# Five reorderings in a two-block model kernel: a state copy, modulation tiles, gb's halves and held loads

## The chip, the cores and the metric

The kernel runs on one core of a Trainium2 chip. The metric is the device time of one launch in microseconds (us); three runs of the kernel before gave 926.8, 927.32 and 931.11, so the median is 927.32 us.

## The reference, cut to what matters

A sequence of 256 tokens of width 1024 goes through three layers. The first is an even mixer (a gated depthwise convolution of 31 taps, layer-normed, beside a gated linear recurrence, LRU, in both directions), the second an odd mixer (pooling over windows of 2, 4, 8 and 16 in rows of 64, grouped matmuls, a gate). The third is a block with its own inputs: chunked HGRN2 attention in both directions, a gated MLP over positions (SGU), then a SwiGLU. All is fp32.

```
for l in range(DEPTH):
    shift, scale, gate = split(silu(c) @ mod_w[l] + mod_b[l], 3)
    hx = modulate(rmsnorm(x, norm_g[l]), shift, scale)
    ...                                  # even_mixer or odd_mixer
    x = x + gate * out_x
# second block
p = h @ w_in                             # f_f, f_b, i, q, og, u, v, ga, gb
o_f, s_f = hgrn2_chunked(qh, k_f, logf_f, vh, s0_f)      # s0: the context's final state
o_b, s_b = hgrn2_chunked(flip(...), s0_b)
o_b_mlp = chunk_sgu(gelu(u), gelu(v), ln_v_g, ln_v_b, w_s, b_s)   # uses layernorm(v)
merged = sigmoid(ga) * (o_a @ w_pa) + sigmoid(gb) * (o_b_mlp @ w_pb)
x = x + mod[2] * (merged @ w_o)
x = x + mod[5] * ((silu(a) * b) @ w_down)                # a, b = split(h2 @ w_up)
out = rmsnorm(x, g_final)
```

The state is carried from chunk to chunk as S = diag(decay) S + d, four chunks of 64 tokens in each direction, and starts from the state that the context leaves.

## The kernel before, in words

Features lie on the partitions, the 256 tokens along the free axis. All weights are one stream of 252 tiles of 128 rows by 1024 columns (512 KB), in the order of `ORDER` (line 72). A tile is named after its product: `xb`, `va`, `vg`, `gate`, `cv`, `ga`, `gb`, `ya`, `yb` in the first layer, `ou`, `og`, `grp`, `oa`, `ob` in the second, `f`, `i`, `q`, `u`, `v`, `o`, `ga2`, `gb2`, `pa`, `pb`, `wo`, `ua`, `ub`, `d0` to `d2` in the third. A tile of most names passes through four engines:

- SyncE loads it into `raw`, a ring of six (line 413), once TensorE has finished the tile six places earlier.
- ScalarE rounds it to `w_hi` (`highs`, line 956), VectorE takes the remainder as `w_lo` (`lows`, line 1370). Both are called by name and index at fixed places of each engine's program and work off all tiles up to the one named.
- TensorE does three matmuls of 256 columns for each of the eight k-tiles (`three`, lines 573 to 575), 24 to a tile, and moves on. `tile_done` counts the tiles.

Each engine's program is written out by hand and runs strictly in order, so a VectorE instruction that waits holds up all that stand behind it, the next `w_lo` too. There is no scheduler; the semaphores alone tie the engines.

The modulation vectors of the later layers (`mod`) are made on VectorE: GpSimd loads 80 tiles `modw` of 512 KB in groups of four (line 452), each slot again when `modw_used` tells that VectorE is done with it; `mod_tiles(g, row, first, n)` (line 1399) multiplies tiles of group g with a row and sums (line 1404).

The places of the change:

- First layer, ga: `lru_root(3, ...)` and `lru_scan(3)` are the recurrence of the last pair of heads, with `lows` for the tiles ga 4 to ga 7 inside.
- First layer, gb: VectorE normalises the convolution (`normalised`), multiplies it with ga (`ya_product`, line 1647) and splits it (`ya_low`, line 1651), beside ScalarE's `conv_silu` and `ya_high`.
- Second layer, ou: TensorE computes ou 0 to 3 side by side, so that these four are finished within a short time and four loads go out together. ScalarE copies each product to `opad` (line 1201), VectorE pools four of them at a time (`pooled`), and multiplies modulation tiles twice (`second_pair`).
- Third layer, the second direction (d = 1): TensorE makes the context's state in `px[0]` (`context_state`, line 802); VectorE copies it to `St` (line 1957). Only then may TensorE write the transposed keys into `px[0]` (`keys(1, 0)`, line 794), which ScalarE copies out (line 1271). Chunk states follow (line 814), then `scores` (line 824). `normalise_v` (from line 1998) is the layer norm of v for the SGU and stands between `decays(1)` and `states(1)`.
- Third layer, up: `mod_tiles(18, 0)` stands ahead of the loop over the 22 pairs ua, ub.

Of the kernel before, what the change touches and what calls it, by code (L numbers as in the profile page):

```python
# [72 lines left out]
TILE = {key: n for n, key in enumerate(ORDER)}  # L73
# [78 lines left out]
def build(nc, ins, out):  # L152
    with ExitStack() as ctx:
# [14 lines left out]
        gb2 = at("gb2", 68, [KT, T])  # L168
# [107 lines left out]
        ga2 = at("ga2", W, [KT, T])  # L276
# [167 lines left out]
        def _(pool):  # L444
# [34 lines left out]

            copies_after = {3: (0,), 5: (1,), 7: (2, 3), 11: (4, 5), 15: (6,), 17: (7,)}  # L480
            for g in range(MOD_TILES // MOD_SLOTS):
                if g == 17:
                    pool.wait_ge(sg_act, 1)
                    add_up([(vn[:, 0, :], v2), (vsq[:, 0, :], vsq)], sg_act, 0, HEADS, 0)
                elif g == 19:
                    add_up([(sq4[:, 0, :], sq4)], sq_ready, 4 * KT, KT - 1)
                for n in range(g * MOD_SLOTS, (g + 1) * MOD_SLOTS):
                    loads(n)
                    for t in copies_after.get(n, ()):
                        shifted_copies(t)  # L490
                if g == 7:
                    add_up([(sq1[:, 0, :], sq1)], sq_ready, 0, KT - 1)
                elif g == 10:
                    add_up([(sqx[:, 0, :], sqx)], sq_ready, KT, KT - 1)
                elif g == 12:
                    add_up([(sq2[:, 0, :], sq2), (sqc[:, 0, :], sqc)], sq_ready, 2 * KT, KT - 1, 2)
# [447 lines left out]
        def _(act):  # L944
# [100 lines left out]
            def silu_out(name, t, dst):  # L1045
                done(name, t)
                act.activation(dst[:, t, :], psum_of(name, t)[:, 0:T], ACT.Silu).then_inc(free_of(name, t), 1)
# [119 lines left out]
            silu_out("gb", 0, gb)  # L1167
            conv_silu(0)
            silu_out("gb", 1, gb)
            conv_silu(1)  # L1170
            ya_high(0)
            ya_high(1)
# [187 lines left out]
        def _(v):  # L1360
# [241 lines left out]
            mod_tiles(3, 1, 2, 2)  # L1602
            lru_scan(2)
            lows("ga", 3)
            mod_tiles(4, 1)
            lru_root(3, ("ga", 5))
            lows("ga", 7)
            mod_tiles(5, 1, 0, 2)
            lru_scan(3)
            lows("gb", 2)  # L1610
            mod_tiles(5, 1, 2, 2)
            mods_used(6)
# [54 lines left out]
            normalised(1)  # L1667
            lows("gb", 5)
            ya_product(0)
            ya_product(1)  # L1670
            v.wait_ge(lru_free, KT)
            yb_product(0, 2)
            lows("gb", 6)
            ya_low(0)
            lows("gb", 7)
            ya_low(1)
# [274 lines left out]
            def states(d):  # L1951

                g0_ = 4 + 10 * d
                order = (0, 1, 2, 3) if d == 0 else (3, 2, 1, 0)
                lows(*(("v", 1) if d == 0 else ("ga2", 5)))
                v.wait_ge(hg_pe, g0_ + 3)
                v.tensor_copy(St[:, order[0], :, :], px[0][:].rearrange("p (h e) -> p h e", h=HEADS)).then_inc(hg_dve, 1)
                for n in range(3):
                    lows(*(("v", 3) if d == 0 else ("ga2", 7)) if n == 0 else (("o", 0) if d == 0 else ("gb2", 0)))
                    v.wait_ge(hg_pe, g0_ + 6 + n)  # L1960
                    if n:
                        S.sync()
                    v.wait_ge(hg_dve, 9 * d + 5 + n)
                    for hd in range(HEADS):
                        c = hd * CHUNKS + order[n]
                        a = v.scalar_tensor_tensor(out=St[:, order[n + 1], hd, :], in0=St[:, order[n], hd, :],
                                                   scalar=dec[:, c:c + 1], in1=px[n % 2][:, hd * P:(hd + 1) * P],
                                                   op0=ALU.mult, op1=ALU.add)
                        if hd == HEADS - 1:
                            a.then_inc(hg_dve, 1)  # L1970
                        else:
                            S.do(a)
                lows(*(("o", 2) if d == 0 else ("gb2", 1)))
                v.wait_ge(hg_pe, g0_ + 9)
                v.wait_ge(in_sgu, 48)
                mask = tri[:, d:d + 1, :].to_broadcast([P, HEADS, P])
                S.do(v.copy_predicated(sc[:, 0:HEADS, :], mask, px[0][:].rearrange("p (r t) -> p r t", t=P)))
                S.sync()
                v.copy_predicated(sc[:, HEADS:, :], mask, px[1][:].rearrange("p (r t) -> p r t", t=P)) \
                 .then_inc(hg_dve, 1)  # L1980
# [12 lines left out]

            def normalise_v():

                lows("ga2", 2)
                v.wait_ge(sd_ready, 8)
                S.do(v.reciprocal(lnv[:, 1, :], lnv[:, 3, :]))
                S.sync()
# [1 line left out]
                def by_token(a):  # L2001
                    return a.rearrange("p (n t) -> p n t", n=1).to_broadcast([P, HEADS, T])

                lows("ga2", 3)
                S.do(tt_(vn[:], v2[:], by_token(lnv[:, 0, :]), ALU.subtract))
                S.sync()
                S.do(tt_(vn[:], vn[:], by_token(lnv[:, 1, :]), ALU.mult))
# [13 lines left out]
            mod_tiles(16, 0)  # L2021
            lows("o", 2)
            decays(1)
            normalise_v()
            states(1)
            mod_tiles(17, 0)

# [74 lines left out]
            rstd(10, v4[:, 0, :], v4[:, 1, :])  # L2102
            modulate(3 * KT, x, v4[:, 1, :], sc3, sh3, t4, h3_hi, h3_lo)
            lows("ub", 2)
            mod_tiles(18, 0)
            for t in range(FT):
                ahead("ua", t)
                emptied(v, "ua", t)
# [4 lines left out]
                S.do(v.tensor_copy(ff_hi[:, t, :], fr))  # L2113
                S.sync()
                v.tensor_tensor(ff_lo[:, t, :], fr, ff_hi[:, t, :].bitcast(F32), ALU.subtract).then_inc(ff_ready, 1)
                if 2 <= t < 6:
                    mod_tiles(19, 0, t - 2, 1)
            mods_used(20)
            S.do(tt_(gate3, mod[:, 9 * KT:10 * KT], col("b_mod_2", 5 * KT, KT), ALU.add))
            S.sync()  # L2120
# [101 lines left out]
```

## Time and profile before

| | before |
|---|---|
| median of three runs | 927.32 us |
| the profiled execution: its own time | 927.22 us |
| its span, first to last instruction | 925.4 us |
| TensorE busy | 893.5 us, 97% of the span |
| VectorE busy | 701.2 us, 76% |
| ScalarE busy | 501.5 us, 54% |
| GpSimd busy | 143.1 us, 15% |
| HBM read | 188.60 MB, 205 GB/s over the span |
| mean granted TensorE clock | 0.993 |

The span is 1.8 us less than the time; that rest lies around it. TensorE's share is high, and matmuls are pipelined, so what counts is where it stands idle and where its clock was lowered: the few stretches of idle time, and who ended each.

### The profile page before, as it was taken

The page shows a single profiled execution, that of the slowest core. Times are in us where ns is not written, and L with a number is a line of the kernel's source. Part 1 is how long each engine was busy: PE and PEld are TensorE (multiplying, and loading weights), DVE is VectorE, ACT ScalarE, POOL GpSimd, SP SyncE. Part 2 cuts the span into 40 slices and gives each one's busy share as a digit, 9 for nine tenths or more (in the row PEclk, how much of TensorE's full clock was granted, in tenths as well). Part 3 has the DMA queues.
Part 4 walks back from the last instruction along what each step waited for, and adds up shares of the span by engine and source line. Part 5 has one row for each costly group of instructions (what it writes and reads, how often), then busy time and mean ns, then how long its engine had stood idle before and what let it go on. Part 6 is the DMA issues. An engine that isn't in the chain of part 4 may idle for free.

```text
span 925.4 us, 17444 instructions
## 1 busy us (share of the span) xinstructions
PE 893.5 (97%) x7172; PEld 838.2 (91%) x7172; DVE 701.2 (76%) x1008; ACT 501.5 (54%) x718; POOL 143.1 (15%) x254
## 2 busy tenths in 40 slices
PE   8999999999999999999999999979999999999996
PEld 7788777689999999989999999969999889999995
DVE  5687578989798999878589975776985786666453
ACT  5475888896744555335544483654544354444441
POOL 0004674710022003200311100300001000000000
PEclk9999999999999999999999999989999999999999
DMA  9934977986685878866628754625565375565661
GB/s 369 369 137 150 313 261 223 276 315 195 199 274 183 299 236 257 296 207 183 185 89 335 243 154 122 224 73 183 169 183 175 136 249 183 183 182 183 201 197 58
DMA packets 55294, 195.44 MB, mean 211 GB/s; under 512 B 7856, under 2 KB 7984, under 8 KB 53808
## 3 DMA queue, kind: packets, MB, share of 16 engines
q1 hardware_dynamic: 39600, 147.73, 49.0%
q0 software_dynamic: 15616, 46.61, 14.7%
q8 instruction: 57, 0.93, 0.4%
q14 instruction: 21, 0.17, 0.1%
HBM read 188.60 MB, written 1.05 MB: 205 GB/s over the span
## 4 chain that ended last, share of the span: by engine, by line
PE 65%; DVE 16%; DMA 6%; ACT 5%; issue 4%; POOL 2%; SPq 0%; DVEq 0%; ACTq 0%; POOLq 0%
PE ps L573 19%; PE ps L575 18%; PE ps L574 18%; DVE w_lo L1370 6%; PE ps L734 3%; DMA raw<-in_stream 2%; DMA m<-in_mod_w 2%; ACT w_hi L956 2%; DMA modw<-in_mod_w 2%; POOL shifts L461 2%; PE px L652 2%; PE ps L663 1%; DVE modw L1404 1%; DVE win L1384 1%; DVE li L1384 1%
## 5 line engine op out<-in xcount | busy, mean ns | idle before, releaser
L1370 DVE TENSOR_TENSOR w_lo<-raw,w_hi 128x1024 fp32r<-128x1024 f32 x232 | 281.0, 1228 | 113.2 <-ACT w_hi L956 112.8
L956 ACT ACTIVATE w_hi<-raw 128x1024 fp32r<-128x1024 f32 x232 | 243.1, 1055 | 114.7 <-DMA raw<-in_stream 113.7
L573 PE MATMUL ps<-h_hi,w_hi 128*128 128x256 f32 (+1 forms) x928 | 274.8, 296 | 13.8 <-DVE w_lo L1370 10.8
L574 PE MATMUL ps<-h_lo,w_hi 128*128 128x256 f32 (+1 forms) x928 | 270.1, 291 | 0.0
L575 PE MATMUL ps<-h_hi,w_lo 128*128 128x256 f32 (+1 forms) x928 | 270.1, 291 | 0.0
L573 PEld LDWEIGHTS ps<-h_hi,w_hi 128*128 128x128 f32 x928 | 178.3, 192 | 24.8 <-DVE w_lo L1370 13.7
L574 PEld LDWEIGHTS ps<-h_lo,w_hi 128*128 128x128 f32 x928 | 178.5, 192 | 3.6 <-issue 1.2
L575 PEld LDWEIGHTS ps<-h_hi,w_lo 128*128 128x128 f32 x928 | 178.4, 192 | 2.6
L573 PE MATMUL ps<-h2o_hi,w_hi 128*128 128x256 f32 x352 | 102.1, 290 | 0.0
L574 PE MATMUL ps<-h2o_lo,w_hi 128*128 128x256 f32 x352 | 100.1, 284 | 0.0
L575 PE MATMUL ps<-h2o_hi,w_lo 128*128 128x256 f32 x352 | 100.0, 284 | 0.0
L452 POOL DMA_DIRECT2D modw<-in_mod_w x80 | 42.8, 537 | 331.3 <-DVE modw L1404 187.4
L1404 DVE SCALAR_TENSOR_TENSOR modw<-modw,c_row 128x1024 f32<-128x1024 f32 x64 | 76.3, 1227 | 7.5 <-DMA modw<-in_mod_w 7.5
L461 POOL DMA_DIRECT2D shifts<-upad x128 | 62.7, 498 | 62.0 <-DVE upad L1523 56.1
L573 PEld LDWEIGHTS ps<-h2o_hi,w_hi 128*128 128x128 f32 x352 | 68.1, 193 | 0.8 <-issue 0.2
L574 PEld LDWEIGHTS ps<-h2o_lo,w_hi 128*128 128x128 f32 x352 | 68.0, 193 | 0.3 <-issue 0.2
L575 PEld LDWEIGHTS ps<-h2o_hi,w_lo 128*128 128x128 f32 x352 | 68.0, 193 | 0.0
L474 POOL TENSOR_TENSOR sq<-sq 128x256 f32<-128x256 f32 x24 | 19.4, 810 | 309.4 <-ACT sq L1185 309.4
L1185 ACT ACTIVATE sq<-x 128x256 f32<-128x256 f32 x32 | 13.4, 418 | 67.6 <-DVE x L1693 67.4
L573 PE MATMUL ps<-ff_hi,w_hi 128*128 128x256 f32 x176 | 49.8, 283 | 0.0
L574 PE MATMUL ps<-ff_lo,w_hi 128*128 128x256 f32 x176 | 49.8, 283 | 0.0
L575 PE MATMUL ps<-ff_hi,w_lo 128*128 128x256 f32 x176 | 49.8, 283 | 0.0
(336 smaller groups left out, 1761.8 us busy)
## 6 DMA issues: line engine op xcount, KB each, us to landing
raw<-in_stream SPq DMA_DIRECT2D x252, 512.0 KB, 3.8
modw<-in_mod_w POOLq DMA_DIRECT2D x80, 512.0 KB, 5.8
m<-in_mod_w SPq DMA_DIRECT2D x8, 1024.0 KB, 19.4
shifts<-upad POOLq DMA_DIRECT2D x128, 35.5 KB, 3.9
c_row<-in_c_rows SPq DMA_DIRECT2D x3, 512.0 KB, 6.6
ctxT<-in_ctxT SPq DMA_DIRECT2D x1, 1024.0 KB, 4.9
x<-in_xT SPq DMA_DIRECT2D x1, 1024.0 KB, 6.9
ctx2T<-in_ctx2T SPq DMA_DIRECT2D x1, 1024.0 KB, 6.3
```

The source lines that it names most:

```text
L452: pool.dma_start(modw[j][:], ins["mod_w"][t]).then_inc(modw_in[j], 16)
L461: pool.dma_start(shifts[t % 2][32 * d:32 * d + 32, g, :], upad[32 * g:32 * g + 32, t % 3, d:d + RW]).then_inc(shifts_in[t % 2], 16)
L474: a = pool.tensor_tensor(dst, src[:, 0, :] if k == 1 else dst, src[:, k, :], ALU.add)
L573: pe.matmul(o, wh, hi, start=start, stop=False)
L574: pe.matmul(o, wh, lo, start=False, stop=False)
L575: return pe.matmul(o, wl, hi, start=False, stop=stop)
L652: mm = pe.matmul(px[b][:, :], w[:, 4 * e + b, :], xpad[:, head, :, SCONV_LEFT:SCONV_LEFT + T], start=True, stop=True)
L734: mm = pe.matmul(o[:, e * T:(e + 1) * T], w[:, 4 * e + k, :], d_in[:, 4 * (t // 2) + k, :], start=(k == 0), stop=(k == 3))
L956: act.activation(w_hi[split[0] % HI_RING][:], raw[n % RING][:], ACT.Copy).then_inc(w_hi_ready, 1)
L1370: v.tensor_tensor(w_lo[n % RING][:], raw[n % RING][:], w_hi[split[0] % HI_RING][:].bitcast(F32), ALU.subtract).then_inc(w_lo_ready, 1)
L1384: return v.tensor_tensor(o, a, b, op)
L1404: v.scalar_tensor_tensor(out=modw[s][:], in0=modw[s][:], scalar=1.0, in1=c_row[:, row, :], op0=ALU.mult, op1=ALU.mult, accum_out=mod[:, t: ...
```

## The change: what it does

1. `states(1)`: the copy of the context's state to `St` now stands ahead of the layer norm of v, not behind it; the calls of `lows` between them are spaced anew (up to ga2 7 inside the loop over chunks, not before it).
2. First half, VectorE: group 4 of the modulation tiles is done as two tiles, then the rest behind `lru_root(3)`; two tiles of group 5 move behind `lru_scan(3)`.
3. gb: ScalarE rounds gb 6 ahead of `conv_silu(1)`; VectorE makes its remainder between the two `ya_product`.
4. ou: GpSimd's loads of group 9 wait until TensorE has finished the tile ou 6.
5. up: group 18's four tiles are no longer done ahead of the loop; the loop takes one tile after each of its steps 2 to 9, groups 18 and 19, where it took group 19 after steps 2 to 5.

```diff
@@ gpsimd: the loop over groups g of modulation tiles
+                if g == 9:
+                    pool.wait_ge(tile_done, TILE[("ou", 6)] + 1)
@@ scalar: gb
             silu_out("gb", 1, gb)
+            highs("gb", 6)
             conv_silu(1)
@@ vector: ga
             lows("ga", 3)
-            mod_tiles(4, 1)
+            mod_tiles(4, 1, 0, 2)
             lru_root(3, ("ga", 5))
             lows("ga", 7)
+            mod_tiles(4, 1, 2, 2)
+            lru_scan(3)
             mod_tiles(5, 1, 0, 2)
-            lru_scan(3)
             lows("gb", 2)
@@ vector: gb
             ya_product(0)
+            lows("gb", 6)
             ya_product(1)
             v.wait_ge(lru_free, KT)
             yb_product(0, 2)
-            lows("gb", 6)
@@ vector: states(d)
-                lows(*(("v", 1) if d == 0 else ("ga2", 5)))
+                lows(*(("v", 1) if d == 0 else ("ga2", 2)))
                 v.wait_ge(hg_pe, g0_ + 3)
                 v.tensor_copy(St[:, order[0], :, :], px[0][:]...)
+                if d:
+                    normalise_v()
                 for n in range(3):
-                    lows(*(("v", 3) if d == 0 else ("ga2", 7)) if n == 0 else (("o", 0) if d == 0 else ("gb2", 0)))
+                    lows(*(("ga2", 5 + n) if d else ("o", 0) if n else ("v", 3)))
...
-                lows(*(("o", 2) if d == 0 else ("gb2", 1)))
+                lows(*(("o", 2) if d == 0 else ("gb2", 0)))
@@ vector: normalise_v()
-                lows("ga2", 2)
+                lows("ga2", 3)
                 v.wait_ge(sd_ready, 8)
                 S.do(v.reciprocal(lnv[:, 1, :], lnv[:, 3, :]))
...
-                lows("ga2", 3)
+                lows("ga2", 4)
@@ vector: around the calls
             decays(1)
-            normalise_v()
             states(1)
@@ vector: up
-            mod_tiles(18, 0)
             for t in range(FT):
...
-                if 2 <= t < 6:
-                    mod_tiles(19, 0, t - 2, 1)
+                if 2 <= t < 10:
+                    mod_tiles(18 + (t - 2) // 4, 0, (t - 2) % 4, 1)
```

How the instructions stand is shown at three places. First VectorE in the third layer, from the remainder of ga2 2 on; `lnv` and `vn` are the layer norm of v. Before:

```order
L1370 TENSOR_TENSOR w_lo_59<-raw_53,w_hi_63 128x1024
L1998 RECIPROCAL lnv<-lnv 128x256
L1370 TENSOR_TENSOR w_lo_60<-raw_54,w_hi_64 128x1024
L1384 TENSOR_TENSOR vn<-v_149,lnv 128x1024
L1384 TENSOR_TENSOR vn<-vn,lnv 128x1024
L2010 TENSOR_SCALAR vn<-vn,cols 128x256 x4
L1370 TENSOR_TENSOR w_lo_55<-raw_49,w_hi_65 128x1024
L1370 TENSOR_TENSOR w_lo_56<-raw_50,w_hi_66 128x1024
L1957 COPY St<-px 128x512
L1370 TENSOR_TENSOR w_lo_57<-raw_51,w_hi_61 128x1024
L1370 TENSOR_TENSOR w_lo_58<-raw_52,w_hi_62 128x1024
```

The same place in the changed kernel, whose line numbers lie three to six higher here:

```order
L1373 TENSOR_TENSOR w_lo_59<-raw_53,w_hi_63 128x1024
L1961 COPY St<-px 128x512
L1373 TENSOR_TENSOR w_lo_60<-raw_54,w_hi_64 128x1024
L2004 RECIPROCAL lnv<-lnv 128x256
L1373 TENSOR_TENSOR w_lo_55<-raw_49,w_hi_65 128x1024
L1387 TENSOR_TENSOR vn<-v_149,lnv 128x1024
L1387 TENSOR_TENSOR vn<-vn,lnv 128x1024
L2016 TENSOR_SCALAR vn<-vn,cols 128x256 x4
L1373 TENSOR_TENSOR w_lo_56<-raw_50,w_hi_66 128x1024
L1972 SCALAR_TENSOR_TENSOR St<-St,small,px 128x128 x4
L1373 TENSOR_TENSOR w_lo_57<-raw_51,w_hi_61 128x1024
```

The copy has moved up by seven rows, and the update of the first chunk (`St<-St,small,px`) now stands behind the layer norm with one `w_lo` between, and the later `w_lo` between the updates.

Second, VectorE in the first layer behind the remainders of ga 2 and ga 3; `li`, `lr` and `asq` belong to the recurrence, `w_lo_59` is ga 4. Before:

```order
L1404 SCALAR_TENSOR_TENSOR modw_67,mod<-modw_67,c_row 128x1024
L1404 SCALAR_TENSOR_TENSOR modw_68,mod<-modw_68,c_row 128x1024
L1404 SCALAR_TENSOR_TENSOR modw_69,mod<-modw_69,c_row 128x1024
L1404 SCALAR_TENSOR_TENSOR modw_70,mod<-modw_70,c_row 128x1024
L1384 TENSOR_TENSOR li<-li,xpad 128x512 x2
L1548 SCALAR_TENSOR_TENSOR lr<-asq_74,lr 128x1024
L1370 TENSOR_TENSOR w_lo_59<-raw_53,w_hi_65 128x1024
L1370 TENSOR_TENSOR w_lo_60<-raw_54,w_hi_66 128x1024
```

And in the changed kernel:

```order
L1407 SCALAR_TENSOR_TENSOR modw_67,mod<-modw_67,c_row 128x1024
L1407 SCALAR_TENSOR_TENSOR modw_68,mod<-modw_68,c_row 128x1024
L1387 TENSOR_TENSOR li<-li,xpad 128x512 x2
L1551 SCALAR_TENSOR_TENSOR lr<-asq_74,lr 128x1024
L1373 TENSOR_TENSOR w_lo_59<-raw_53,w_hi_65 128x1024
L1373 TENSOR_TENSOR w_lo_60<-raw_54,w_hi_66 128x1024
L1387 TENSOR_TENSOR li<-li,xpad 128x512 x2
L1551 SCALAR_TENSOR_TENSOR lr<-asq_75,lr 128x1024
L1373 TENSOR_TENSOR w_lo_55<-raw_49,w_hi_61 128x1024
L1373 TENSOR_TENSOR w_lo_56<-raw_50,w_hi_62 128x1024
L1407 SCALAR_TENSOR_TENSOR modw_69,mod<-modw_69,c_row 128x1024
L1407 SCALAR_TENSOR_TENSOR modw_70,mod<-modw_70,c_row 128x1024
```

Two of four modulation tiles have moved from ahead of ga 4's remainder to behind ga 7's.

Third, ScalarE at gb; `w_hi_63` is gb 6, `ya_hi` needs VectorE's `ya_product`. Before:

```order
L1155 ACTIVATE conv<-conv,cols 128x256 x4
L1047 ACTIVATE gb<-ps 128x256
L1155 ACTIVATE conv<-conv,cols 128x256 x4
L1161 ACTIVATE ya_hi<-conv 128x1024 x2
L956 ACTIVATE w_hi_63<-raw_51 128x1024
```

And in the changed kernel:

```order
L1157 ACTIVATE conv<-conv,cols 128x256 x4
L1049 ACTIVATE gb<-ps 128x256
L958 ACTIVATE w_hi_63<-raw_51 128x1024
L1157 ACTIVATE conv<-conv,cols 128x256 x4
L1163 ACTIVATE ya_hi<-conv 128x1024 x2
```

The rounding of gb 6 has moved ahead of four silu and of both `ya_hi`; gb 7's still follows them.

## Rows read from the trace of the kernel before

**Rows 1.** The page: busy time of each engine.
```profile
PE 893.5 (97%) x7172; PEld 838.2 (91%) x7172; DVE 701.2 (76%) x1008; ACT 501.5 (54%) x718; POOL 143.1 (15%) x254
```

**Rows 2.** Waits of TensorE: who for whom, us in total, times, longest.
```profile
PE ps L573 <- DVE w_lo L1370: 10.8, 8, 3.2
```

**Rows 3.** Windows: stretch, length, busy of PE, PEld, DVE, ACT, POOL, clock, DMA share, GB/s.
```profile
775.00:800.00 25.00, 25.00 (x211) 25.00 (x210) 15.22 (x22) 11.18 (x14) 0.00 (x0) 1.00 0.58 182
...
560.00:576.00 16.00, 16.00 (x135) 15.49 (x135) 8.47 (x18) 6.52 (x10) 0.00 (x0) 1.00 0.41 118
...
614.00:618.00 4.00, 4.00 (x20) 4.00 (x21) 1.50 (x2) 2.14 (x3) 0.00 (x0) 0.50 0.01 4
...
195.00:199.00 4.00, 4.00 (x23) 4.00 (x23) 4.00 (x6) 3.97 (x6) 0.00 (x0) 0.59 0.52 207
```

**Rows 4.** Timeline of TensorE, third layer: start, length, instruction, [idle before, who ended it].
```profile
602.65 1.95 PE L802 MATMUL px<-vtok,kdT 128*128 128x128 f32 x16
...
613.86 1.97 PE L794 MATMUL px<-cols,Kk 128*128 128x128 f32 x8 [6.39 <-DVE St L1957]
```

**Rows 5.** Timeline of VectorE, the same stretch.
```profile
604.12 1.74 DVE L1998 RECIPROCAL lnv<-lnv 128x256 f32<-128x256 f32 x1
...
609.55 1.38 DVE L2010 TENSOR_SCALAR vn<-vn,cols 128x256 f32<-128x256 f32 x4
...
613.12 0.68 DVE L1957 COPY St<-px 128x512 f32<-128x512 f32 x1
...
620.89 1.12 DVE L1966 SCALAR_TENSOR_TENSOR St<-St,small,px 128x128 f32<-128x128 f32 x4 [2.22 <-PE px L814]
```

**Rows 6.** Timeline of ScalarE, the same stretch.
```profile
609.92 0.38 ACT L1277 ACTIVATE ga<-ps 128x256 f32<-128x256 f32 x1
```

**Rows 7.** Timelines of the first layer at ga: VectorE, ScalarE, TensorE.
```profile
187.29 1.23 DVE L1404 SCALAR_TENSOR_TENSOR modw<-modw,c_row 128x1024 f32<-128x1024 f32 x1 [1.13 <-DMA modw<-in_mod_w]
...
189.71 1.22 DVE L1404 SCALAR_TENSOR_TENSOR modw<-modw,c_row 128x1024 f32<-128x1024 f32 x1 [1.19 <-DMA modw<-in_mod_w]
...
193.21 2.35 DVE L1370 TENSOR_TENSOR w_lo<-raw,w_hi 128x1024 fp32r<-128x1024 f32 x2
...
187.57 1.34 ACT L1080 ACTIVATE lr<-lr,small 128x512 f32<-128x512 f32 x2
...
194.48 0.39 PE L573 MATMUL ps<-h_hi,w_hi 128*128 128x256 f32 x1 [2.07 <-DVE w_lo L1370]
```

**Rows 8.** Timelines of the first layer at gb: VectorE, ScalarE, TensorE.
```profile
227.18 1.22 DVE L1370 TENSOR_TENSOR w_lo<-raw,w_hi 128x1024 fp32r<-128x1024 f32 x1
...
232.74 1.23 DVE L1370 TENSOR_TENSOR w_lo<-raw,w_hi 128x1024 fp32r<-128x1024 f32 x1 [1.47 <-ACT w_hi L956]
...
231.67 1.04 ACT L956 ACTIVATE w_hi<-raw 128x1024 fp32r<-128x1024 f32 x1
...
234.02 0.38 PE L573 MATMUL ps<-h_hi,w_hi 128*128 128x256 f32 x1 [2.09 <-DVE w_lo L1370]
```

**Rows 9.** Timelines of the second layer at ou: VectorE, ScalarE, TensorE.
```profile
309.55 2.35 DVE L1370 TENSOR_TENSOR w_lo<-raw,w_hi 128x1024 fp32r<-128x1024 f32 x2
...
318.03 1.26 DVE L1384 TENSOR_TENSOR win<-opad 128x1056 f32<-128x1056 f32 x1 [1.38 <-ACT opad L1201]
...
316.58 1.05 ACT L956 ACTIVATE w_hi<-raw 128x1024 fp32r<-128x1024 f32 x1
...
323.46 0.39 PE L573 MATMUL ps<-h_hi,w_hi 128*128 128x256 f32 x1 [0.86 <-DVE w_lo L1370]
```

**Rows 10.** Up: timelines of ScalarE and TensorE, then loads issued at 732.5:734 and 748:758, median us to landing.
```profile
740.22 1.06 ACT L956 ACTIVATE w_hi<-raw 128x1024 fp32r<-128x1024 f32 x1 [6.50 <-DMA raw<-in_stream]
...
742.58 0.39 PE L573 MATMUL ps<-h_hi,w_hi 128*128 128x256 f32 x1 [3.17 <-DVE w_lo L1370]
...
raw<-in_stream SPq DMA_DIRECT2D x4, 512.0 KB, 10.4
...
raw<-in_stream SPq DMA_DIRECT2D x4, 512.0 KB, 3.7
```

## The prediction

> **What bounds the kernel now.** I read the busy shares first [rows 1]: TensorE works 97% of the span, so a change that adds no matmul and removes none can only win where TensorE stands idle or runs at its lower clock. Then TensorE's waits [rows 2]: eight waits for a `w_lo` of VectorE sum to 10.8 us. The timeline adds one single wait of 6.39 us for the copy of `St` [rows 4]. Then the windows [rows 3]: the granted clock is 1.00 (2.4 GHz) in steady work, but 0.50 (1.2 GHz) from 614 to 618, right behind that wait, and 0.59 on average from 195 to 199, right behind a wait of 2.07 [rows 7]. From the steady window one matmul of 256 columns takes 25/211 = 0.12 us, so a tile of 24 takes 2.88 us; I call that one tile. Everything below is read from the timelines around the idle times. Times are on the clock of the kernel before; a place that moves earlier moves everything behind it, because the loads, ScalarE and VectorE mostly wait for TensorE's finished tiles.
>
> **Part 1, the state copy.** TensorE ends ga2 2 at 613.86 - 6.39 = 607.47 and waits for the copy, which ends at 613.12 + 0.68 = 613.80 [rows 4, 5]. What the copy reads is complete at 602.65 + 1.95 = 604.60 [rows 4]. In its new place it stands behind the remainder of ga2 2 alone, which is done when the reciprocal starts in the old order, about 604.2, so it runs from 604.7 to 605.4, two us before TensorE asks. The 6.39 us go. With them goes the lower clock: TensorE worked at 0.50 from 613.86 to just past 618, some 4.2 us, of which half, 2.1 us, was lost [rows 3].
>
> What is late next: the second chunk state waits for the first update of `St`, which now stands behind the layer norm. VectorE: 605.4, plus one `w_lo` of 1.17 (half of 2.35, [rows 7]), then the stretch from the reciprocal to the last `vn` with one `w_lo` in it, 609.55 + 1.38 - 604.12 = 6.8 [rows 5], one more `w_lo`, and the update of 1.12 [rows 5]: 615.6. TensorE: keys from 607.5, about 1.0 (half of the 1.97 at half clock, [rows 4]), a tile, a chunk state of about 1.2 (an estimate from the keys and the `context_state` rows, [rows 4]), a tile: 615.5. A dead heat; the wait is 0 to 0.5. ScalarE is free of ga2's outputs at 609.92 + 0.38 = 610.3 [rows 6] and needs about 1.1 for the two copies of the keys, until 611.4, where TensorE comes at 611.4: 0 to 0.2. The later remainders, ga2 6 and 7, stand between the updates and are made while TensorE runs the tiles. I take 0.2 for all of it: part 1 gives 6.39 + 2.1 - 0.2 = 8.3 us. Bounds: 5.9 (the clock falls all the same and the wait is 0.5) and 8.5.
>
> **Parts 2 and 3, ga and gb, belong together.** At ga VectorE waits 1.13 and 1.19 us for landing modulation tiles [rows 7], then makes ga 4's remainder at 193.21, and TensorE stands from 192.41 to 194.48. With two of the tiles moved behind, VectorE is free at 187.29 - 1.13 = 186.2, at `lr` by 187.5 after two short products, and waits there for ScalarE's `lr`, done at 187.57 + 1.34 = 188.9 [rows 7]; `lr` takes 1.14 and ga 4's remainder is ready at 191.3, before 192.41. The wait of 2.07 goes, and probably the half clock behind it: (1 - 0.59)/0.5 x 4 = 3.3 us at 1.2 GHz, 1.6 lost [rows 3]. But VectorE itself gains little: of its 2.3 us of idle time 1.4 comes back as the wait for `lr` and some 0.5 at ga 6 and 7. It is ahead by 0.4 us from there to gb.
>
> At gb that is the limit. The remainder of gb 5 is done at 227.18 + 1.22 = 228.4; TensorE begins gb 5 at 234.02 - 2.09 - 3.0 = 228.9 [rows 8]. So only 0.5 us of room, plus the 0.4: TensorE can be at most 0.9 to 1.0 earlier here, whatever it gained at ga; the rest turns into waits of about 1.8 at gb 4 and 0.5 at gb 5. Next, gb 6: its rounding started at 231.67, behind `ya_hi` [rows 8]; now it is done by about 227, the remainder comes behind the first `ya_product`, at 230.2, and TensorE, there at 230.9, does not wait. The 2.09 go. But gb 7's rounding still stands behind the second `ya_hi`, and that now waits for a `ya_product` that is one `w_lo` later. On ScalarE: about 232.6 to 233.7, the remainder at 234.9, and TensorE is there at 233.8: a new wait of 1.2. VectorE's idle 1.47 [rows 8] is what pays. Sum: 1.0 + 2.1 - 1.2 = 1.9 us. Bounds: 0 (gb 7 and the yb tiles behind take it all) and 2.07 + 1.6 + 2.09 = 5.8.
>
> **Part 4, ou.** Only the second of two waits can go: the first remainder, ou 6, starts at 309.55 without idle time before it, VectorE being busy with other work [rows 9], so a load that lands sooner changes nothing there. The second, 0.86 us, ends with a chain: ScalarE rounds ou 11 at 316.58 to 317.63 because the loads came late, and only then copies ou 7 to `opad`, for which VectorE waits 1.38 [rows 9]. TensorE ended ou 7 at 323.46 - 0.86 - 2 x 2.88 = 316.8. With the loads of group 9 out of the way the copy can come at 316.9 rather than 317.5: 0.6 us. The four held loads then go out together at ou 6's end, when the tiles from ou 12 on are loaded, whose remainders are not due for 10 us. Bounds: -0.4 and 0.86.
>
> **Part 5, up.** TensorE stands 3.17 us for ua 3, whose load waits behind and beside four modulation tiles: four raw loads issued near 733 land after 10.4 us (median), lone ones after 3.7; ScalarE waits 6.50 for the first of them [rows 10]. Group 19's loads followed directly on `mod_tiles(18, 0)`; now they are issued one by one from step 2 of the loop on. The first raw load then lands after 3.7 to 5 us, I take 4.2: 732.6 + 4.2, rounding 1.1, remainder 1.3, gives 739.2, and TensorE asks at 742.58 - 3.17 = 739.4. The part gives 3.0 us; bounds 1.9 and 3.2. The eight tiles in the loop cost VectorE 1.2 each; with two `w_lo` (2.35) and three small steps of about 0.4 a step of the loop takes 4.7, and TensorE needs 5.76 for its two tiles: covered. If that cover went, each step would cost what is over.
>
> **Sum.** 8.3 + 1.9 + 0.6 + 3.0 = 13.8 us. The profiled execution took 927.22 us, its span 925.4 and the rest around it unchanged: 913.4. The median of the runs is 927.32, so it stands for it.
>
> **A rule against it.** The row first: in the first direction the same transposes, chunk states and tiles run from 560 to 576 without an idle gap at a clock of 1.00 [rows 3]; so the fall behind the 6.39 us is the wait's. The Trainium skill, "TensorE: Matmul & The Clock Gate", section "Part 4: PE-mode transpose", says that transposes do not count as busy for the clock as other matmuls do. By that rule the clock could still fall in this stretch. The trace does not bear it out where the transposes stand among tiles.
>
> **Rivals.**
> - The clock falls anyway, in the second direction or behind the new waits at gb 4. For: 2.07 us of idle time were followed by it at ga. Against: the wait of 3.17 us at up had no such fall, and the window of the first direction. Without part 1's 2.1 us the time is 915.5; with a stretch like that of 195 to 199 as well, 917.1.
> - VectorE is no limit at gb, TensorE keeps all of ga's gain: 5.8 for 1.9, so 909.5. Against: 0.5 us of room at gb 5, and VectorE has no idle time ahead of it.
> - Parts 2 and 3 do not do what they say: what ga gives back is waited for at gb 4 to gb 7 and at yb, 0 for 1.9: 915.3; if up also gives only its lower bound, 916.4.
> - Slower than before: the held loads. The fifth `second_pair` takes a tile of group 9 right behind the remainders of ou 10 and 11, of which the first lets TensorE go at 323.46 [rows 9], so about 324.5; ou 12's remainder stands behind it. The load now goes out at ou 6's end, 316.8 - 2.88 = 314. It costs from the point where landing takes more than 10.5 us, the 10.4 of [rows 10] being the longest median that I saw. To eat 13.8 us the landing would have to take 24 us; the time is then 927.8 or more.
>
> **How the numbers follow.** Forecast 0.60, clock 0.13, no limit at gb 0.08, no gain at ga and gb 0.15, slower 0.02, and 0.02 for gains lost in places that I do not see. The likeliest gives 913.4. The range goes from 910.3, short of the second rival, to 917.3, which takes in the clock and the third rival; about 2 in 10 stay outside. What a measurement of this kernel tells from no change is 0.5%, 4.6 us. Faster by more than that: 0.96; within: 0.03; slower: 0.01.
>
> **What would show it.** Part 1: no wait before the keys in the second direction, clock 1.00 there, at most 0.5 us before a chunk state. Parts 2 and 3: no wait at ga 4, but waits for `w_lo` at gb 4, gb 5 and gb 7 of 2 to 4 us together. Part 4: the second of ou's two waits shrinks to 0.3, the first stays. Part 5: the wait at ua 3 is under 0.5, and the raw loads near it land in 4 to 6 us. I am wrong if TensorE's idle time falls by much less than 12 us, or if a new lower clock shows.

## The result, and the profile after

The changed kernel takes 912.68 us in the median of 4 runs (912.52 to 913.89), the kernel before 927.06 (4 runs, 926.76 to 931.11). The ratio is 0.983, with a 95% interval of 0.981 to 0.985. The forecast was 913.4. The profiled execution took 912.54 us, 14.68 less than that of before.

The page's line of busy times ([rows 1] before), then windows around the places of [rows 7], [rows 8], [rows 4] and [rows 10] (columns as in [rows 3]):

```profile
PE 889.2 (98%) x7172; PEld 834.0 (92%) x7172; DVE 699.6 (77%) x1008; ACT 500.7 (55%) x718; POOL 142.5 (16%) x254
```
```profile
186.00:200.00 14.00, 14.00 (x151) 12.25 (x151) 13.09 (x17) 13.91 (x23) 1.59 (x3) 1.00 0.78 266
220.00:240.00 20.00, 16.79 (x136) 16.21 (x135) 19.29 (x19) 15.58 (x25) 0.00 (x0) 1.00 0.70 216
...
604.00:624.00 20.00, 19.88 (x169) 19.30 (x168) 18.68 (x31) 10.89 (x18) 1.00 (x2) 1.00 0.40 112
725.00:745.00 20.00, 20.00 (x169) 20.00 (x168) 18.05 (x27) 10.78 (x13) 1.62 (x3) 1.00 0.85 279
```

The clock is 1.00 in all four places, and TensorE is busy in three of them but for 0.12 us; gb (220 to 240) has 3.2 us of idle time. The waits there and in ou, by the timeline, and the sums over the kernel, by the view of waits (us in total, times, longest):

```profile
223.78 0.39 PE L575 MATMUL ps<-h_hi,w_hi 128*128 128x256 f32 x1 [1.09 <-DVE w_lo L1373]
227.31 0.39 PE L575 MATMUL ps<-h_hi,w_hi 128*128 128x256 f32 x1 [0.39 <-DVE w_lo L1373]
232.17 0.36 PE L575 MATMUL ps<-h_hi,w_hi 128*128 128x256 f32 x1 [1.73 <-ACT gb L1049]
...
308.81 0.39 PE L575 MATMUL ps<-h_hi,w_hi 128*128 128x256 f32 x1 [0.94 <-DVE w_lo L1373]
320.81 0.39 PE L575 MATMUL ps<-h_hi,w_hi 128*128 128x256 f32 x1 [0.23 <-DVE w_lo L1373]
```
```profile
PE ps L575 <- DVE w_lo L1373: 4.3, 7, 1.1
...
PE ps L575 <- ACT gb L1049: 1.7, 1, 1.7
```

The waits for `w_lo` fell from 10.8 us [rows 2] to 4.3. A new one of 1.73 has come, at gb 6, and it is for ScalarE. Where the 14.68 us come from can be read off SP's queue: the load of a raw tile goes out when the tile six places ahead of it is done, so its issue times are the ends of TensorE's tiles. From one tile's end to another's, in us:

| from the end of | to the end of | before | changed | again | difference |
|---|---|---|---|---|---|
| ga 3 | gb 3 | 37.36 | 33.72 | 33.72 | -3.64 |
| gb 3 | gb 7 | 13.85 | 15.46 | 15.59 | +1.61 |
| gb 7 | ou 0 | 63.02 | 62.88 | 62.96 | -0.14 |
| ou 0 | ou 10 | 23.55 | 22.91 | 22.91 | -0.64 |
| ou 10 | ga2 2 | 280.87 | 280.87 | 280.90 | 0 |
| ga2 2 | ga2 7 | 34.92 | 26.58 | 26.59 | -8.34 |
| ga2 7 | ua 2 | 94.14 | 94.04 | 93.97 | -0.10 |
| ua 2 | ua 3 | 9.19 | 5.76 | 5.76 | -3.43 |
| ua 3 | d2 0 | 114.63 | 114.48 | 114.48 | -0.15 |

("Again" is a second profile of the changed kernel, below.) With the changed kernel 0.15 us later at the end of ga 3 the differences sum to 14.68. For the experiments too I read these rows: a part shows in its own, whatever happens elsewhere.

### The profile page after: what moved, and what is told of

Read it like the earlier page. It is cut to its first block, busy times and chain, and to the rows that moved or that the text cites. A ratio compares the mean times of both kernels' runs of the same rounds, so it can differ in the third digit from the quotient of the medians.

```text
span 910.7 us, 17445 instructions
## 1 busy us (share of the span) xinstructions
PE 889.2 (98%) x7172; PEld 834.0 (92%) x7172; DVE 699.6 (77%) x1008; ACT 500.7 (55%) x718; POOL 142.5 (16%) x254
## 4 chain that ended last, share of the span: by engine, by line
PE 78%; DVE 11%; ACT 4%; DMA 3%; issue 2%; SPq 0%; DVEq 0%; ACTq 0%
PE ps L575 22%; PE ps L577 22%; PE ps L576 22%; PE ps L736 3%; DVE w_lo L1373 3%; PE px L654 2%; DMA m<-in_mod_w 2%; PE ps L665 2%; DMA raw<-in_stream 1%; DVE win L1387 1%; ACT w_hi L958 1%; PE px L841 1%; DVE modw L1407 1%; PE px L816 1%; ACT la L1078 1%
```

## The experiments

Each ratio is against the kernel before as it ran on the same chip beside the variant. Its median there was 929.38 us (16 runs) for parts 1, 2 and 3, and 5 alone and for the first try of the filled waits. It was 929.33 (7 runs) for the changed kernel again, part 4 undone, the tiles later and the first move of the pairs, and 927.96 (19 runs) for the others. The ratio is taken over all runs and can lie 0.001 or so from the quotient of the medians.

**The changed kernel again**, beside its variants on one chip.

> The changed kernel itself once more, so that the variants of it beside it have a run of the same chip to stand against. Expected: its first profile again, TensorE's gb 7 some 1.9 us and its end 14.7 us earlier than in the kernel before, the three waits at gb 4, 5 and 6 of 1.1, 0.4 and 1.7 us, no stretch at a clock of 0.50 before the end. If one of the waits of 2 us or more brings a lower clock with it in this execution, as one did in the kernel with part 1 alone, the time is some 1.7 us longer.

912.98 us (912.98 to 913.52), ratio 0.983 (0.981 to 0.985). The medians differ by 16.4 us here, by 14.4 in the result: it is the kernel before that varies, by up to 6.6 us, and the last section says with what. The rows repeat within 0.13 us, and so do the three waits at gb (1.22, 0.39, 1.72).

**Part 1 alone**, with the calls of `lows` spaced as in the changed kernel (not shown).
```diff
             decays(1)
-            normalise_v()
             states(1)
...
                 v.tensor_copy(St[:, order[0], :, :], px[0][:].rearrange("p (h e) -> p h e", h=HEADS)).then_inc(hg_dve, 1)
+                if d:
+                    normalise_v()
```


> The kernel before with part 1 alone: in the second direction the copy of St stands ahead of the layer norm, and the remainders around it are placed as in the changed kernel. My theory: the wait of 6.39 us before the keys goes, and with it the stretch at a clock of 0.50 (2.1 us), 0 to 0.3 us comes back before the chunk states. The time falls by 8.3 us, to about 918.9; TensorE has no idle time of over 0.5 us between 600 and 625 and the clock is 1.00 there. Rival 1 (the clock falls for the transposes, not for the wait): 5.9 to 6.4 us, so 920.9 to 921.3, with a stretch at 0.50 near 608. Rival 2 (the four parts help each other, and alone part 1 is worth clearly less because something later takes it back): above 921.5, with new idle time of TensorE behind 625.

919.93 us, ratio 0.991 (0.989 to 0.992). From ga2 2 to ga2 7: 26.57 us, 8.35 less than before, with nothing else changed. The windows of this kernel:

```profile
604.00:624.00 20.00, 19.88 (x168) 19.30 (x167) 18.25 (x30) 11.95 (x18) 0.00 (x0) 1.00 0.42 129
734.00:738.00 4.00, 4.00 (x23) 4.00 (x22) 3.00 (x5) 3.10 (x4) 0.00 (x0) 0.57 0.95 385
```
Rival 1 is out: with the wait gone, the same transposes run at 1.00. But the whole execution gained 7.7 and not 8.3 us. The second row says why in the main: the clock fell behind the wait at ua 3, which is 2.75 us here. In the profile of before a wait of 3.17 at that place had no such fall. Step ua 2 to ua 3 took 10.24 us for 9.19.

**The waits filled.** Order of before; TensorE multiplies a matrix of ones into an unread bank while it waits. The first try (32 and 96 such matmuls) was far too long; the second has 9 and 28.
```diff
+            keep_busy(9, bank_of("ga", 4))
             for t in range(4, KT):
                 thirds("ga", t, *own)
...
             thirds("ga2", 2, *own2)
+            keep_busy(28)
             pe.wait_ge(hg_dve, 14)
```


> The kernel before, with the two waits left where they are but filled with matmuls whose results nobody reads: 32 of 128 columns (some 1.9 us) before ga 4, 96 (some 5.8 us) before the second keys of the second direction. It leaves nothing out. My theory: the lower clock belongs to the idle time, so both stretches at 0.50 go while the order of work stays. At the keys 2.1 us are gained; at ga 1.6 are gained and 0 to 1.0 of it stays behind gb, where VectorE is the limit. The time falls to 924.2 to 925.2. Rival 1 (transposes and chunk states do not hold the clock): the stretch near 611 to 618 at 0.50 stays, time 926.2 to 927.3. Rival 2 (the added matmuls hold up the tile behind them): a gain of less than 1 us with no idle time before the tiles.

942.21 us, ratio 1.014. A filler in f32 is two instructions of 0.11 us, so 96 took 21.6 us, and rival 2 held trivially. Useful all the same: the last keys came 21.6 us of filler later and no clock fell; from gb 3 to gb 7, VectorE now far ahead, took 11.52 us, four tiles without a wait.

> The kernel before with the two waits filled with matmuls again, now sized by the filler's measured length (96 of them took 21.6 us): 9 before ga 4 (2.0 us) and 28 before the second keys of the second direction (6.3 us). It leaves nothing out. My theory: both waits stay in length, filled, and the two stretches at 0.50 go, since they belong to the idle time. Behind the keys 2.1 us are gained; behind ga 4 1.6 are gained and at most 1.0 of it is left at the first ou tile, VectorE being the limit at gb. Time 2.1 to 3.1 us below the kernel before of the same chip, ga2 2 to gb2 7 done in 59.3 us and not 61.5. Rival (the transposes and chunk states do not hold the clock): a stretch at 0.50 near 614, and no gain there.

927.00 us (923.57 to 927.61, 10 runs), ratio 0.998 (0.996 to 1.000). Timeline and windows:

```profile
607.29 6.42 PE L602 MATMUL px<-ones_p 128*128 128x128 f32 x56
```
```profile
192.00:200.00 8.00, 8.00 (x74) 7.82 (x67) 8.00 (x9) 7.97 (x14) 0.00 (x0) 1.00 0.82 303
233.00:237.00 4.00, 4.00 (x25) 4.00 (x25) 4.00 (x4) 3.37 (x5) 0.00 (x0) 0.65 0.16 66
604.00:624.00 20.00, 19.87 (x170) 19.17 (x169) 15.22 (x23) 10.95 (x16) 0.00 (x0) 1.00 0.30 90
740.00:746.00 6.00, 5.33 (x25) 5.34 (x26) 4.52 (x7) 4.40 (x5) 0.00 (x0) 0.50 0.82 334
```
Both stretches at the lower clock are gone where the idle time is filled: ga2 2 to ga2 7 takes 32.98 us, 1.94 less than before, and ga 3 to gb 3 takes 35.73, 1.63 less. So of part 1's 8.34 us, 6.39 are idle time and 1.95 go with filling it. The profiled execution gained nothing in the end, since the clock fell in two other places, behind waits of 2.43 us at gb 6 and 3.25 us at ua 3, which are not filled. That was in neither theory.

**Parts 2 and 3 alone.**
```diff
-            mod_tiles(4, 1)
+            mod_tiles(4, 1, 0, 2)
             lru_root(3, ("ga", 5))
             lows("ga", 7)
+            mod_tiles(4, 1, 2, 2)
+            lru_scan(3)
             mod_tiles(5, 1, 0, 2)
-            lru_scan(3)
...
             silu_out("gb", 1, gb)
+            highs("gb", 6)
             conv_silu(1)
...
             ya_product(0)
+            lows("gb", 6)
             ya_product(1)
             v.wait_ge(lru_free, KT)
             yb_product(0, 2)
-            lows("gb", 6)
```


> The kernel before with parts 2 and 3 alone (modulation tiles of ga moved behind, the halves of gb 6 sooner). My theory, corrected by the profile of the changed kernel: ga gives back 2.07 us of waiting and 1.6 of half clock, but VectorE is ahead by 0.4 us only, so that most comes back as waits at gb 4, gb 5 and gb 6, 3.2 us together, the last for the PSUM bank that ScalarE's output of gb 2 frees; gb 7 does not wait. The time falls by 1.9 us, to 925.3. Rival 1 (TensorE keeps what ga gives): 5.8 us, 921.4, and no wait at gb. Rival 2 (it is all given back by the yb tiles): 927.2 at the end, TensorE's gb 7 earlier but its first ou tile not.

927.12 us, the median of 10 runs, nine of them from 924.65 to 927.92 and one of 2232.5, of which the cause is not known; ratio 0.998 (0.997 to 1.000). The profiled execution took 924.65, 2.57 less than that of before. ga 3 to gb 3: 33.72; gb 3 to gb 7: 15.49; together 49.21 against 51.21, a gain of 2.0. The wait for ScalarE at gb 6 is there at 1.72 us. The stage itself varies, though. In the order of before it took 51.22, 51.14, 50.93 and 52.14 us (before, part 1 alone, part 5 alone, part 5's loads alone). In the changed order it took 49.18, 49.31 and 49.21, but 50.93 in the kernel with part 4 undone, below. The means differ by 1.7 us, single executions by 0 to 3.

**Part 4 undone** in the changed kernel.
```diff
-                if g == 9:
-                    pool.wait_ge(tile_done, TILE[("ou", 6)] + 1)
```


> The changed kernel without part 4 (group 9's loads are not held back). My theory: the second wait in ou, at ou 10, grows from 0.23 us to 0.6 to 1.0 again (it is 0.86 before and 0.59, 1.05 and 0.66 in the kernels with parts 2 and 3, 1 and 5 alone), nothing else changes, and the time is 0.4 to 0.8 us longer than the changed kernel's. Rival (the wait shrank because the work at ou came earlier, or by chance, not for the loads): the wait stays at 0.2 to 0.4 and the time stays the same.

913.85 us (912.75 to 915.29), ratio 0.984 (0.982 to 0.986); against the changed kernel's 912.98 the times alone decide nothing. The row does:

```profile
323.41 0.38 PE L573 MATMUL ps<-h_hi,w_hi 128*128 128x256 f32 x1 [0.71 <-DVE w_lo L1371]
```
The wait is 0.71 for 0.23, and ou 0 to ou 10 takes 23.39 us for 22.91. With the hold and this order in ou the row is 22.91 to 22.92 us (4 executions). Without it, it is 23.29 to 23.73 in seven; the eighth, the kernel with the long filler, whose loads go out at other times against VectorE, had 22.92. So the hold is worth 0.4 to 0.8 us where the loads collide. Chance alone would hardly give the short row four times out of four with the hold and once out of eight without it. This execution lost another 1.75 us between ga 3 and gb 7, where its VectorE waited 2.50 us for `lr` of ScalarE, and the changed kernel's 0.77. ScalarE in turn had stood 4.38 us for the load of ga 4, and 2.65 in the changed kernel. That load took 7.6 us to land for 5.9, though it went out at the same place. Why it took longer is open; this was far ahead of the place where part 4 acts. In this execution the start of `lr`, and with it VectorE's work behind it, hung on this landing, and of what parts 2 and 3 give in the others little was left.

**Part 5 alone, and its loads alone.** The second keeps group 18's tiles ahead of the loop. Part 5 alone:
```diff
             lows("ub", 2)
-            mod_tiles(18, 0)
...
-                if 2 <= t < 6:
-                    mod_tiles(19, 0, t - 2, 1)
+                if 2 <= t < 10:
+                    mod_tiles(18 + (t - 2) // 4, 0, (t - 2) % 4, 1)
```
and its loads alone, where GpSimd waits ahead of group 19:
```diff
                     add_up([(sq4[:, 0, :], sq4)], sq_ready, 4 * KT, KT - 1)
+                    pool.wait_ge(tile_done, TILE[("ua", 2)] + 1)
...
-                if 2 <= t < 6:
-                    mod_tiles(19, 0, t - 2, 1)
+                if 6 <= t < 10:
+                    mod_tiles(19, 0, t - 6, 1)
```


> The kernel before with part 5 alone (group 18's modulation tiles into the loop too, so that group 19's loads go out one by one). My theory: the wait of 3.17 us at ua 3 goes, raw loads near it land in 4 to 6 us, and the time falls by 3.0 to 3.2 us, to about 924.1; VectorE's eight tiles in the loop cost nothing. Rival (VectorE is short in the loop, and what the load gives is lost at later tiles of up as waits for w_lo): gain under 1.9 us, above 925.3, with waits for w_lo between 745 and 780.

> The kernel before with group 19's loads alone changed: GpSimd issues them once ua 2 is done, and VectorE works them off in steps 6 to 9 of the loop; group 18's four modulation tiles stay ahead of the loop. It tells whether the 3.43 us of part 5 are the transfer's or VectorE's. My theory (four raw tiles and four modulation tiles in flight together are what made raw loads land after 10 us): ua 3 follows ua 2 after 5.8 us and not 9.2, the gain is 3.2 to 3.5 us, as with the whole of part 5, and the raw loads issued near 733 land after 4 to 6 us. Rival (VectorE's 4.9 us of modulation tiles ahead of the loop are what held up the remainder of ua 3): less than 1 us gained.

Part 5 alone: 923.09 us, ratio 0.995 (0.993 to 0.996). Its loads alone: 923.83 us, ratio 0.996 (0.994 to 0.998). In both, ua 3 ends 5.76 us behind ua 2, with no wait. Landing of the four raw loads of [rows 10], first with part 5, then with its loads alone:

```profile
raw<-in_stream SPq DMA_DIRECT2D x4, 512.0 KB, 5.0
```
```profile
raw<-in_stream SPq DMA_DIRECT2D x4, 512.0 KB, 5.8
```
They took 10.4 before. VectorE's four modulation tiles ahead of the loop cost nothing; it is the traffic of group 19 beside the raw loads. In the kernel before, the DMA engines were busy all the time in the windows from 737 to 745 (share 1.00 to 1.02, at 365 to 416 GB/s), which hold TensorE's idle time of 739.4 to 742.6. From ua 3 on, 114.48 us against 114.63: the eight tiles in the loop are hidden.

**VectorE's work ahead of gb made less.**
```diff
-            mod_tiles(5, 1, 2, 2)
-            mods_used(6)
-            S.do(tt_(gate0, mod[:, 0:KT], col("mod_b", 2 * KT, KT), ALU.add))
-            affine_cols(sc1, shift1, col("norm_g", KT, KT), "mod_b", 3 * KT, KT)
-            S.sync()
...
             yb_low(1, 0, 5)
+            mod_tiles(5, 1, 2, 2)
+            mods_used(6)
+            S.do(tt_(gate0, mod[:, 0:KT], col("mod_b", 2 * KT, KT), ALU.add))
+            affine_cols(sc1, shift1, col("norm_g", KT, KT), "mod_b", 3 * KT, KT)
+            S.sync()
```


> The changed kernel with the last two modulation tiles of group 5, gate0 and the shift and scale columns that are made of them moved from ahead of the layer norm to behind the first yb_lo, where VectorE waits 3.87 us for ScalarE anyway; the loads of two tiles of group 6 go out later with them. My theory (VectorE's amount of work ahead of gb is the limit): VectorE is 2.9 us earlier from the layer norm on, the waits at gb 4 and gb 5 (1.09 and 0.39) go, and that at gb 6 (1.73, for the bank of gb 2) goes as well since ya_hi and ScalarE's output of gb 2 come 2.8 us earlier; up to 0.5 stays at gb 7. Gain 2.7 to 3.2 us against the changed kernel: 909.5 to 910.0. Rival 1 (the waits at gb 4 and 5 are for landing loads and not for VectorE): gain under 1 us. Rival 2 (the bank wait stays because it hangs on ScalarE's order): 1.5 us, 911.2. Rival 3 (the two loads that go out later are late for the tiles of group 6): VectorE waits near 252 and yb 0's output frees its bank late; gain given back behind yb.

909.96 us, ratio 0.980 (0.978 to 0.981). gb 3 to gb 7: 12.56 us for 15.59, 3.0 less. The waits at gb 4 and gb 5 are gone, and of the wait for the bank 0.82 is left:

```profile
229.52 0.35 PE L575 MATMUL ps<-h_hi,w_hi 128*128 128x256 f32 x1 [0.82 <-ACT gb L1049]
```
VectorE's amount of work is the limit at gb 4 and 5; at gb 6 it is VectorE and ScalarE's order together, between my theory and rival 2. Rival 3 falls: nothing is given back behind yb (62.90 us).

**The bank freed sooner**, on top of that.
```diff
             ya_high(0)
+            silu_out("gb", 2, gb)
             ya_high(1)
-            for t in range(2, KT):
+            for t in range(3, KT):
```


> The kernel with the modulation tiles later, and ScalarE's output of gb 2, which frees the PSUM bank that gb 6 needs, moved from behind the second rounding of ya to between the two. My theory: the wait of 0.82 us at gb 6 goes (the bank is free at about 227.2, TensorE asks at 228.7) and at most 0.1 comes back at gb 7; gain 0.7 to 0.8 us against the kernel with the tiles later alone, 909.2. Rival (the rounding of gb 7 or the second ya_lo is late next): a wait for w_lo or for ya_lo of 0.5 us or more at gb 7 or ya 0, gain under 0.3.

908.99 us, ratio 0.980 (0.977 to 0.982), the same ratio as for the kernel without this step, which was timed on another chip. The times alone do not show the gain; the row does. No wait at gb 6; gb 3 to gb 7 takes 11.92 us, 0.64 less. In the two kernels without this step it took 12.56 and 12.91 (the latter in the next paragraph), in the two with it 11.92 and 11.52. This confirms the mechanism: gb 6 goes into the bank of gb 2 and waited for the output that stood behind both roundings of `ya` on ScalarE.

**The pairs in ou**, a miss and then a gain. On top of the tiles later:
```diff
-            second_pair(2)
             pooled(0)
             lows("ou", 7)
+            second_pair(2)
             second_pair(3)
```
and, in place of that, on top of the bank freed sooner:
```diff
-            second_pair(2)
             pooled(0)
             lows("ou", 7)
-            second_pair(3)
+            second_pair(2)
             lows("ou", 9)
             pooled(1)
             lows("ou", 11)
-            second_pair(4)
+            second_pair(3)
...
-            pairs_after = {1: 5, 2: 6, 4: 7, 5: 8, 7: 9, 8: 10, 10: 11, 11: 12, 14: 13}
+            pairs_after = {1: 4, 2: 5, 4: 6, 5: 7, 7: 8, 8: 9, 10: 10, 11: 11, 13: 12, 14: 13}
```


> The kernel with the modulation tiles later (the run above), and in ou the third pair of modulation tiles moved from ahead of the first pooling to behind the remainder of ou 7. My theory: the remainder of ou 6 now waits for ScalarE's rounding of a raw tile that lands at about 304.5, and not for VectorE, so the first wait in ou (0.94 us) goes and 0 to 0.3 comes back at ou 8 to ou 12. Gain 0.6 to 0.9 us against the kernel with the tiles later, 908.8 to 909.3 in all. Rival (VectorE's total of work from ou 4 to ou 12 is the limit, so that the wait only moves to ou 10 or ou 12): no gain, with a wait of 0.8 us or more there.

911.74 us, ratio 0.981 (0.980 to 0.983): 1.8 slower than without the move. The wait at ou 6 went, and a larger one came two tiles later, as two pairs stood together ahead of ou 8's remainder:

```profile
313.30 0.38 PE L575 MATMUL ps<-h_hi,w_hi 128*128 128x256 f32 x1 [1.79 <-DVE w_lo L1373]
```
ou 10 waited another 0.42. The row ou 0 to ou 10 is 1.03 us longer (23.95); another 0.6 of the loss lies between ga 3 and gb 7, where nothing was changed.

> The kernel above (bank freed sooner), and two of the five pairs of modulation tiles in ou moved behind: the third to behind the remainder of ou 7, the fourth to behind that of ou 11, the fifth into og's loop, where the pairs take steps 1, 2, 4, 5, 7, 8, 10, 11, 13 and 14. Moving the third alone made it 1.5 us slower, since two pairs then stood together ahead of the remainder of ou 8. My theory (VectorE's amount of work ahead of each remainder decides, and og has room): the wait of 0.94 us at ou 6 shrinks to 0 to 0.3, that at ou 8 does not come, ou 10 waits 0.2 to 0.4; gain 0.5 to 0.9 us against the kernel above, 908.4 to 908.7. Rival (og has no room: its steps with a pair take VectorE 3.7 us to TensorE's 2.9): waits for w_lo between 340 and 385, no gain or a loss of up to 1.5 us.

907.51 us (907.34 to 907.62), ratio 0.978 (0.975 to 0.980): the fastest of all. The changed kernel, in another session, had 912.98 and 0.983 (0.981 to 0.985); the two profiles differ by 5.5 us, of which the rows of gb and ou hold 5.25. gb 3 to gb 7 takes 11.52 us, four tiles without a wait; ou 0 to ou 10 takes 21.73 for 22.91, with no wait at ou 6 and 0.23 at ou 10; og, behind it, loses nothing. TensorE's waits for `w_lo` over the whole kernel sum to 1.9 us. A window of og:

```profile
340.00:385.00 45.00, 44.54 (x351) 43.55 (x350) 43.96 (x55) 19.15 (x35) 13.85 (x16) 1.00 0.82 273
```
VectorE is busy 98% of that window and TensorE still waits 0.40 us only. So og has next to no room left.

## Why the prediction was right, step by step

The mechanisms and their sum were right, 13.8 us forecast and 14.68 measured; one step named the wrong releaser.

**Part 1**, 8.3 forecast, 8.34 measured. The copy runs from 601.97 to 602.66, 2.0 us before TensorE asks at 604.64, and the first update at 611.58:

```profile
601.97 0.69 DVE L1961 COPY St<-px 128x512 f32<-128x512 f32 x1 [0.44 <-PE px L804]
```
```profile
611.58 1.12 DVE L1972 SCALAR_TENSOR_TENSOR St<-St,small,px 128x128 f32<-128x128 f32 x4
```
On the old clock, 2.66 us later there, the update starts at 614.24; the forecast was 615.6 - 1.12 = 614.5. No chunk state waits for it, and `kdT` costs 0.12. The 2.1 put down to the clock is 1.94 by the filled wait, and a part of that is not the clock's (see part 5).

**Parts 2 and 3**, 1.9 forecast, 2.03 measured, but by another route. Right: the wait at ga 4 and the half clock behind it go, VectorE waits for `lr` instead (it starts at 188.30), ga 4's remainder is done at 190.6 (191.3 forecast), and waits come at gb 4 and gb 5. They are 1.09 and 0.39 for 1.8 and 0.5, because VectorE is not 0.4 us ahead but 1.3: the remainder of gb 5 is done at 227.26, 228.40 before, on a clock that runs 0.15 late here. Wrong: "The remainder comes behind the first `ya_product`, at 230.2, and TensorE, there at 230.9, does not wait." The remainder was done at 229.53, and TensorE did wait, for the PSUM bank:

```profile
228.42 1.06 ACT L1163 ACTIVATE ya_hi<-conv 128x1024 fp32r<-128x1024 f32 x1 [0.19 <-DVE conv L1651]
230.69 1.06 ACT L1163 ACTIVATE ya_hi<-conv 128x1024 fp32r<-128x1024 f32 x1 [1.21 <-DVE conv L1651]
231.66 0.36 ACT L1049 ACTIVATE gb<-ps 128x256 f32<-128x256 f32 x1
```
ScalarE stands 1.21 us for the second product, which VectorE now makes one remainder later, and then empties gb 2's bank. I had followed this very chain to gb 7's rounding and not asked what else stands behind it. Hence no wait at gb 7 (1.2 forecast) but 1.73 at gb 6; both come from the late second `ya_hi`. The sum also took 1.2 for a difference of 234.9 - 233.8 = 1.1. TensorE ended gb 5 1.6 us earlier for 1.0 forecast (230.44 for 231.93, on a clock that is 0.15 late), and waited 1.73 for 1.2. The two errors, 0.6 gained and 0.5 lost, nearly cancel: that the term came out at 2.03 is luck. The rival without a limit at gb, 5.8 us, was reached only with VectorE's work moved and the bank freed: from ga 3 to gb 7 the last version takes 45.24 us, 6.0 less than before.

**Part 4**, 0.6 forecast, 0.64 measured in the changed kernel and 0.48 by undoing it. The wait at ou 6 stayed, as said, since VectorE is busy; the two experiments on pairs show that it is a matter of VectorE's amount of work and not of this one instruction's place.

**Part 5**, 3.0 forecast with an upper bound of 3.2; 3.43 measured. The term that was mis-sized is the idle time itself. In four executions the step from ua 2 to ua 3 took 9.19, 8.86, 8.42 and 5.76 us with waits of 3.17, 2.85, 2.42 and none: each wait cost 0.24 to 0.26 more than the idle time that the timeline shows. If the idle time at the keys cost as much on top, some 1.7 of the 1.94 us are the clock's there; that is an estimate. The four parts together measured 14.44 us for 13.8; another 0.24, net, is in the other rows of the table.

**The signs.** TensorE's idle time fell from 31.9 us (925.4 - 893.5) to 21.5, which is 10.4, and its busy time by 4.3, as the stretches at the lower clock went. The sign set beforehand, "much less than 12 us" of idle time, was too high for the forecast's own terms: 13.8 less the 2.1 and 1.6 of the clock is 10.1. The forecast also stood on one execution of the kernel before, with a lower clock behind two of its four long waits. In executions where it fell more often the change is worth more (16.4 us of medians, above), so a part of the closeness of 913.4 to 912.68 is owed to that execution; the terms are borne out by the rows, one by one.

**The clock rival**, 0.13: it did not come in either profile of the changed kernel, whose longest wait is 1.73 us. The rule of the Trainium skill that I weighed, "TensorE: Matmul & The Clock Gate", section "Part 4: PE-mode transpose", is not borne out here: transposes among tiles, or behind 6.4 us of filler, had a clock of 1.00 in every execution in which the idle wait of 6.39 us was gone. The tiles around them may have kept the clock up; transposes by themselves were not tried.

## What to carry over

When a step on a busy engine is moved, list everything that stands in order behind it on the next engine, and for each ask both what data and which buffer it gives back; a PSUM bank is released by the engine that empties it. A wait removed upstream is worth only the slack of the engine that feeds the next stage, so take work off that engine (3.0 us more here) rather than only reorder it (2.0). Count a wait of TensorE of two microseconds or more as its idle time, plus 0.25, plus a chance (six of twelve here) of some 1.7 us for the clock.

## What the runs showed of the hardware

A wait does not fix whether the clock falls. Idle times of TensorE and whether a stretch at 0.50 followed, over all profiles: 6.39 us, four of four; between 1.99 and 3.25 us, six of twelve, at one and the same place sometimes (ua 3: 2.75 and 3.25 with it, 2.42, 2.85 and 3.17 without; gb 6: 2.43 with it twice, 2.43, 2.09 and 2.11 without; ga 4: 2.07 and 1.99 with it); 1.8 us or less, never, between the kernel's first 60 us and its last tiles. Between the ends of tiles, such a stretch cost 1.5 to 2.3 us. It goes with the spread of the times: beside each other on one chip, the kernel before, with four waits of 2 us or more, ran in 925.2 to 931.7 us (19 runs), the last version, with none above 1.2 after its start, in 907.34 to 907.62 (4). Of those 19 runs the five with a mean granted clock of 0.993 took 925.2 to 927.6 us, the five with 0.988 took 930.1 to 931.7. On the two other chips the same holds in the main, with one exception (0.993 and 930.17).

A wait filled with matmuls costs its filler's length and no more (6.42 us of it, 6.40 between the ends of the tiles), where an idle one costs 0.25 on top. And an f32 filler of 128 columns takes 0.22 us, while a matmul of the stream takes 0.12 for 256.
